# Second attention: the query heads' root moved into the exponential, their rotation moved into the projection

## The reference

```python
q_l = apply_rope_2(rms_norm(split_heads(qkv[..., :Q_DIM], N_HEADS), q_norm_g), cos, sin)
k_l = apply_rope_2(rms_norm(split_heads(qkv[..., Q_DIM:Q_DIM + KV_DIM], N_KV_HEADS), k_norm_g), cos, sin)
k_all = jnp.concatenate([k_c, k_l], axis=2)
s = jnp.einsum('bkgqd,bktd->bkgqt', qg, k_all, ...) * (hd ** -0.5)
p = jax.nn.softmax(s, axis=-1)
o = jnp.einsum('bkgqt,bktd->bkgqd', p, v)
y_lat = merge_heads(o) @ w_o

def rms_norm(x, g):
    return x * lax.rsqrt(jnp.mean(x * x, axis=-1, keepdims=True) + 1e-6) * g
def apply_rope_2(x, cos, sin):
    x1, x2 = jnp.split(x, 2, axis=-1)
    return jnp.concatenate([x1 * cos - x2 * sin, x2 * cos + x1 * sin], axis=-1)
```

## Time and profile before

| | |
|---|---|
| Three runs | 2569.39, 2569.93 and 2573.72 us, median 2569.93 |
| Profiled execution | span 2571.0 us, from its first to its last instruction; no other time is given for it |
| PE busy | 2465.7 us, 96% of the span |
| DVE busy | 1849.9 us, 72% |
| ACT busy | 1103.7 us, 43% |
| Mean granted clock of TensorE | 0.984 of 2.4 GHz |

### The profile page before, as it was taken

The page is one execution under the profiler, slowest core; times in us unless marked ns, Lnnn a source line. Parts: engine busy times, 40 slices in busy tenths (PEclk is TensorE's granted clock), DMA queues, the critical chain, the costliest instruction groups (busy, mean ns, idle before and its releaser), DMA issues.

```text
span 2571.0 us, 39389 instructions
## 1 busy us (share of the span) xinstructions
PE 2465.7 (96%) x15574; PEld 2235.4 (87%) x15574; DVE 1849.9 (72%) x3597; ACT 1103.7 (43%) x1650; POOL 0.2 (0%) x4
## 2 busy tenths in 40 slices
PE   4999999989999999999999999999999999998998
PEld 3998989989989888788888998888998888877998
DVE  7888988878877745768787669896785444676655
ACT  3444565444453324724232652232642322645444
POOL 0000000000000000000000000000000000000000
PEclk8999999999999999999999999999999999999999
DMA  8886766758856531654444266676273333212663
GB/s 317 301 268 222 252 213 229 257 191 274 292 179 203 186 98 51 216 155 129 148 135 127 83 193 208 191 236 198 97 256 131 115 107 96 79 61 74 197 192 104
DMA packets 161384, 453.68 MB, mean 176 GB/s; under 512 B 17713, under 2 KB 21297, under 8 KB 161201
## 3 DMA queue, kind: packets, MB, share of 16 engines
q1 hardware_dynamic: 161200, 451.16, 54.1%
HBM read 450.04 MB, written 1.05 MB: 175 GB/s over the span
## 4 chain that ended last, share of the span: by engine, by line
PE 78%; DVE 5%; ACT 2%; issue 1%; DMA 1%; ACTq 0%; DVEq 0%; SPq 0%
PE PS L1182 25%; PE PS L1184 24%; PE PS L1183 24%; DVE own L1671 1%; PE PS L1209 1%; PE PS L1336 1%; PE PS L1207 1%; PE PS L1382 1%; DVE X L1652 0%; PE PS L1365 0%; ACT Uh L1462 0%; ACT own L1401 0%; DMA SCR<-in_ma 0%; ACT NT L1466 0%; PE PS L1310 0%
## 5 line engine op out<-in xcount | busy, mean ns | idle before, releaser
L1182 PE MATMUL PS<-Uh,own 128*128 128x256 f32 (+1 forms) x2064 | 655.3, 317 | 43.5 <-DVE Ul L1752 20.5
L1183 PE MATMUL PS<-Ul,own 128*128 128x256 f32 (+1 forms) x2064 | 644.6, 312 | 0.0
L1184 PE MATMUL PS<-Uh,own 128*128 128x256 f32 (+1 forms) x2064 | 644.3, 312 | 0.0
L1401 ACT ACTIVATE own<-raw 128x1024 fp32r<-128x1024 f32 x425 | 444.1, 1054 | 360.5 <-PE PS L1184 300.6
L1671 DVE TENSOR_TENSOR own<-raw,own 128x1024 fp32r<-128x1024 f32 x425 | 515.5, 1219 | 68.0 <-ACT own L1401 67.7
L1182 PEld LDWEIGHTS PS<-Uh,own 128*128 128x128 f32 x2064 | 399.5, 194 | 72.7 <-issue 36.5
L1183 PEld LDWEIGHTS PS<-Ul,own 128*128 128x128 f32 x2064 | 400.7, 194 | 19.9 <-issue 0.2
L1184 PEld LDWEIGHTS PS<-Uh,own 128*128 128x128 f32 x2064 | 400.3, 194 | 20.1
L1182 PE MATMUL PS<-Hh,own 128*128 128x256 f32 (+1 forms) x1096 | 348.5, 318 | 1.0 <-DVE own L1671 0.6
L1184 PE MATMUL PS<-Hh,own 128*128 128x256 f32 (+1 forms) x1096 | 343.9, 314 | 0.0
L1183 PE MATMUL PS<-Hl,own 128*128 128x256 f32 (+1 forms) x1096 | 343.9, 314 | 0.0
(11 more groups left out here) (222 smaller groups left out, 3875.4 us busy)
## 6 DMA issues: line engine op xcount, KB each, us to landing
MODS<-in_mm SPq DMA_DIRECT2D x168, 256.0 KB, 3.5
SCR<-in_mm SPq DMA_DIRECT2D x136, 256.0 KB, 3.8
raw<-in_f0i SPq DMA_DIRECT2D x64, 512.0 KB, 4.1
raw<-in_f1i SPq DMA_DIRECT2D x56, 512.0 KB, 3.6
raw<-in_f2i SPq DMA_DIRECT2D x56, 512.0 KB, 3.6
SCR<-in_ma SPq DMA_DIRECT2D x88, 256.0 KB, 5.1
raw<-in_w1i SPq DMA_DIRECT2D x44, 512.0 KB, 4.9
raw<-in_w2i SPq DMA_DIRECT2D x44, 512.0 KB, 4.5
```

What stands on the lines that cost most here:

```text
L1182: e.matmul(o, ll, rh, start=start, stop=False)
L1183: e.matmul(o, lh, rl, start=False, stop=False)
L1184: return e.matmul(o, lh, rh, start=False, stop=stop)
L1401: e.activation(parts(w.n)[0], raw[:, w.n % RING, :], ACT.Copy).then_inc(s["whi"].tell(w.n), 1)
```

## The change

A query head is no longer multiplied by its reciprocal root. A score is linear in the query, so the factor is one per query token, and in the scores the queries lie on the partitions, where `inv_of` already is. It becomes the scale operand of the exponential, one value per partition, and the maximum is scaled by it too. The factor 128 ** -0.5 goes into the same number: the mean is replaced by the sum and the 1e-6 by 128 times it. The norm weight `qn` becomes the scale of ScalarE's copy of the head. So query heads pass neither `spread` nor `headnorm`, and their rotation needs the copied head alone; it is put when the next chunk opens. The key heads keep all their steps. The sine product's buffer is now `NT[:, 1]`, taken in turn by the rotations in their order.

```diff
+    def turn_head(slot):
+        p.put("rope2", f=slot, k=len(p.turned), bank=p.bank())
+        p.turned.append(slot)
+
+    def norm_head(slot, rope):
+
+        p.put("spread", f=slot)
+        p.later(1, lambda: p.put("headnorm", f=slot, bank=p.bank()))
+        if rope:
+            p.later(2, lambda: turn_head(slot))
...
     for t_ in range(8):
         heads(t_, t_, LAT)
+        p.later(1, lambda t_=t_: turn_head(t_))
         if t_ == 0:
             p.put("roots", f=8)
         if 1 <= t_ < 5:
-            by_chunk(norm_head(8 + t_ - 1, t_ - 1, (t_ - 1) % 2 == 0))
+            norm_head(8 + t_ - 1, (t_ - 1) % 2 == 0)
         if t_ == 6:
             p.put("roots", f=0)
-            by_chunk(norm_head(0, 0, True))
-        if t_ == 7:
-            by_chunk(norm_head(1, 1, True))
     p.flush()
     p.put("roots", f=4)
-    for f in norm_head(2, 2, True):
-        f()
...
-        if i % 2 and i // 2 + 3 < 8:
-            steps[i // 2 + 3] = norm_head(i // 2 + 3, i // 2 + 3, True)
-        for h in sorted(steps):
-            steps[h].pop(0)()
...
...
-                    on.wait_ge(s["head_x"], w.f)
+                    if w.f < 8:
+                        on.wait_ge(s["qk2_x"], w.f)
+                    else:
+                        on.wait_ge(s["head_x"], w.f)
...
-                    e.activation(head_of(w.f), PS[:, b, lo:hi], ACT.Copy).then_inc(s["qk2_x"].tell(w.f), 1)
+                        e.activation(head_of(w.f), PS[:, b, lo:hi], ACT.Copy, scale=vec("qn")).then_inc(
...
-                    e.activation(P2[:, w.k % 3, :], PS[:, b, :], ACT.Exp, bias=sm[:, 0:1], scale=float(P) ** -0.5,
-                                 accum_out=sm[:, 1:2]).then_inc(s["prob2"].tell(w.k), 1)
+                    e.activation(P2[:, w.k % 3, :], PS[:, b, :], ACT.Exp, bias=sm[:, 0:1],
+                                 scale=inv_of(w.k // 2)[:, w.k % 2:w.k % 2 + 1], accum_out=sm[:, 1:2]).then_inc(s["prob2"].tell(w.k), 1)
...
-                    e.tensor_scalar(inv_of(w.f), PS[:, b, 0:2], 1.0 / P, 1e-6, ALU.mult, ALU.add).then_inc(
+                    mean = 1.0 if w.f < 8 else 1.0 / P
+                    e.tensor_scalar(inv_of(w.f), PS[:, b, 0:2], mean, mean * P * 1e-6, ALU.mult, ALU.add).then_inc(
...
-                    dst, g = head_of(w.f), NT[:, 0, w.f % 2, :]
+                    dst, g = head_of(w.f), NT[:, 1, w.k % 2, :]
+                    if w.k >= 2:
+                        on.wait_ge(s["roped2"], plan.turned[w.k - 2])
...
-                    e.tensor_scalar(sm[:, 0:1], sm[:, 0:1], -float(P) ** -0.5, None, ALU.mult).then_inc(
-                        s["weight2"].tell(("max", w.k)), 1)
+                    on.wait_ge(s["root_inv"], w.k // 2 - w.k // 2 % 4)
+                    e.tensor_scalar(sm[:, 0:1], sm[:, 0:1], inv_of(w.k // 2)[:, w.k % 2:w.k % 2 + 1], -1.0, ALU.mult,
+                                    ALU.mult).then_inc(s["weight2"].tell(("max", w.k)), 1)
```

More of the change, by code:

```diff
@@ L167, in __init__ @@
         self.last = None
+        self.turned = []
     def put(self, what, **fields):
@@ L887, in schedule @@
         if 1 <= t_ < 5:
-            by_chunk(norm_head(8 + t_ - 1, t_ - 1, (t_ - 1) % 2 == 0))
+            norm_head(8 + t_ - 1, (t_ - 1) % 2 == 0)
         if t_ == 6:
             p.put("roots", f=0)
-            by_chunk(norm_head(0, 0, True))
-        if t_ == 7:
-            by_chunk(norm_head(1, 1, True))
     p.flush()
     p.put("roots", f=4)
-    for f in norm_head(2, 2, True):
-        f()
-    n2, steps = 16, {}
+    n2 = 16
     for i in range(n2 + 3):
@@ L902, in schedule @@
             p.put("score2", k=i, bank=p.bank())
-        if i % 2 and i // 2 + 3 < 8:
-            steps[i // 2 + 3] = norm_head(i // 2 + 3, i // 2 + 3, True)
-        for h in sorted(steps):
-            steps[h].pop(0)()
-            if not steps[h]:
-                del steps[h]
         if 1 <= i <= n2:
@@ L1580, in scalar @@
                     on.wait_ge(s["matmul"], last_mix)
-                    e.activation(head_of(w.f), PS[:, b, lo:hi], ACT.Copy).then_inc(s["qk2_x"].tell(w.f), 1)
+                    if w.f < 8:
+                        on.wait_sem(s_vecs, 16)
+                        e.activation(head_of(w.f), PS[:, b, lo:hi], ACT.Copy, scale=vec("qn")).then_inc(
+                            s["qk2_x"].tell(w.f), 1)
+                    else:
+                        e.activation(head_of(w.f), PS[:, b, lo:hi], ACT.Copy).then_inc(s["qk2_x"].tell(w.f), 1)
                     on.wait_ge(s["matmul"], ("sums", last_tally(w.id), KT - 1))
@@ L1955, in vector @@
                         on.wait_ge(s["matmul"], ("headnorm", f))
-                        if f < 8 or f % 2 == 0:
-                            on.wait_ge(s["roped2"], f)
                     e.tensor_tensor(NT[:, 0, w.f % 2, :].rearrange("p (t n) -> p t n", t=2),
@@ L1965, in vector @@
                     on.wait_ge(s["qk2_x"], w.f)
-                    e.scalar_tensor_tensor(out=dst, in0=dst, scalar=vec("qn" if w.f < 8 else "kn"), in1=PS[:, b, 0:S],
+                    e.scalar_tensor_tensor(out=dst, in0=dst, scalar=vec("kn"), in1=PS[:, b, 0:S],
                                            op0=ALU.mult, op1=ALU.mult).then_inc(s["head_x"].tell(w.f), 1)
```

## The result

| | before | after |
|---|---|---|
| Runs | 21 | 21 |
| Median | 2573.22 us | 2569.16 us |
| Ratio of the runs | | 0.9984, 95% interval 0.9979 to 0.9990 |
| Span of the profiled execution | 2571.0 us | 2568.4 us |
| Projection: first squares of the stage (key heads') to the end of the last chunk | 37.15 us | 40.39 us |

The kernel is 4.1 us faster by the medians, 2.6 to 5.4 by the interval (2573.22 x 0.0010 and x 0.0021), and 3.66 us faster in the stage that was changed. The prediction was 3.2 us, taken off a base of three runs (2569.93). The stage is counted from the first small product of the squares (L1343 before, L1334 after), 2238.00 before and 2238.88 after; the 0.88 ahead of it comes from identical instructions.

What follows compares the result with a forecast made beforehand. TensorE was taken to bound projection and the loop's head work, a chain of waits (5.04 us per turn) the loop without it. +3.5 - 5.9 - 0.8 = -3.2 us, from 2569.93, gave 2566.7 us, range 2562.5 to 2571.

Steps and rivals of the forecast that it cites:

- Rotation behind projection: Between projection chunks: each rotation waits for ScalarE's copy and starts 0.80 us behind its chunk; +3.5 us in sum.
- Entry: From T, the last chunk's end, to the first exponential: T + 4.4 instead of T + 10.36, -5.9 us.
- Rival F: Before the first exponential: the table costs 1.28 us beyond its load, exponential at T + 5.7, kernel 2568.0 us; chance 0.08.
- Loop: Attention loop: head work leaves, 2.56 us per iteration instead of 2.69; -0.8 us.
- the ring: Attention loop: chain maximum, exponential, copy, value sum, transpose, score two iterations on; 5.04 us per turn, 5.12 after the change.
- Rival B: Before the loop: TensorE's clock falls again, 3.4 us at that pace lose 1.5; 2568.2 us, chance 0.18.
- Rival C: Attention loop: the chain of waits is no bound, iterations run at 2.35 us; 2564.4 us, chance 0.13.
- Rival D: Projection: ScalarE's weight conversion delays the head copies, eight rotations wait 1.05 us more, +8.4; 2575.1 us, chance 0.07.
- E: Whole kernel: gain and stalls cancel, as with an entry of -5.0 and a loop at +0.3; 2568.7 to 2570 us, chance 0.06.

Runs made afterwards that it cites:

- e2: Changed kernel with each query head rotated two chunks behind its own instead of one; 2565.30 us, ratio 0.9970 to the kernel before.
- e5: Changed kernel with heads 0 and 1 rotated two chunks behind their own, heads 2 to 7 inside the loop; 2565.32 us, ratio 0.9967.
- e3: Changed kernel with the constant 128 ** -0.5 again in exponential and maximum, without the column; 2568.51 us, ratio 0.9978.
- e6: Changed kernel with the weighted sum of the values put one iteration later; 2563.24 us, ratio 0.9960.
- e9: Kernel before the change with the weighted sum of the values put one iteration later; 2569.53 us, ratio 0.9983.
- e4: Changed kernel with query heads rotated at their old places, the root still the exponential's scale; 2564.84 us, ratio 0.9970.

## Why the prediction was right

- *Rotation behind projection*, +3.5 predicted, +3.24 measured. Gap by gap, from the distances between the squares' products: behind chunk 0 +1.25 (predicted +1.3), behind 1 +0.49 (+0.6), behind 2 and 4 together +0.85 (+0.9), behind 3 +0.82 (+0.9), behind 5 +0.81 (+0.9), behind 6 -0.98 (-0.9). The rotation starts 0.82 behind the end of chunks 1 and 6 and 0.73 behind that of 3 and 5; 0.80 was predicted. e2 shows the cause.
- *Entry*, -5.9 predicted, -5.91 measured. The exponential started 0.01 us behind the end of the table's load, T + 4.45. The scaled maximum was there at T + 4.18 (4.2 predicted), so the load did end last. e5 bears this out: with the root 0.95 us earlier the exponential came 0.80 earlier. Rival F, and with it the drain of 1.38 us that the Trainium skill adds (ScalarE: Activation LUTs, What ACT_TABLE_LOAD costs), does not show in this trace: 0.02 us lie ahead of the load and 0.01 behind it.
- *Loop*, -0.8 predicted, -0.99 measured. The pace is 2.555 us against 2.56. e3 shows that both columns are in the ring at 0.15 us per turn, e6 that the ring is the bound, e9 that before it was TensorE with the head work. TensorE's own need was taken as 2.26 us per iteration; e6 shows 2.19. This changed nothing in the sum, as the ring set the pace.
- The sum was predicted as -3.2 and is -3.66 in the stage: 0.26 less cost in the projection and 0.19 more gain in the loop.
- Rival B did not happen: the mean clock is 1.00 in both windows, while 0.92 and 0.98 stood there before. Rival C (pairs at 4.7) is out by the rows of the loop; it would have taken the open ring of e6. Rival D is out: the idle time ahead of a rotation is 0.23 to 0.56 us, never a conversion (1.05 us) longer. E does not hold either: its entry of -5.0 and loop at +0.3 were -5.91 and -0.99.
- What the prediction did not ask was whether both halves of the change help. Its own terms, +3.5 for the moved rotations and a ring of 2.56 us per iteration over 2.26 us of TensorE's work, pointed to the answer that e4 gave: the second half is a loss of 2.8 us.
- Of the 4.1 us between the medians 3.7 are accounted for. The remaining 0.4 is within the interval, and the stages around are the same instructions (242.9 before and 243.1 us after, behind the last value product).

## What to carry to other kernels

Before work is taken out of a loop, follow the chain across iterations: if it comes back to where it began after n iterations, its length over n is a floor that only work taken out of the chain itself lowers (0.15 us per turn in e3), and consuming a result one iteration later can lift it (7.2 us here, with the same instructions). Where such a ring leaves an engine idle, small work is nearly free there (e4 paid 1.05 us once, in the first turn), and the same work is paid in full in a stage which that engine fills; so price a moved instruction at both places. An operation that needs another engine's copy of the result just made belongs one step further behind, not directly after it.

## What the runs showed of the hardware

A scale with one value per partition in place of a constant costs ScalarE about 0.09 us at both widths seen: 382 to 475 ns for outputs of 256 elements per partition, 688 to 777 for 512. On VectorE one element per partition goes from 154 to 214 ns; that operation also got a second multiplication, but the earlier trace rows has 293 and 349 ns, 0.06 us as well, and there the multiplication by such a value is the only one. In e3 both are taken out of the chain of waits and each turn of it gets shorter by 0.15 us, so they are paid once per turn.
